# Zeroing a token table early in both of its rows, and adding the first-choice rows of h in PSUM for the last two expert pairs

## The reference

```python
def hier_moe(u, ...):                      # u = RMSNorm(h); 4 groups of 8 experts
    ...                                    # best group, then the best two experts in it
    top_w = softmax(top_logit) * g_w       # two weights per token
    hdn = silu(xb @ w1[e]) * (xb @ w3[e])  # per expert, on the tokens that chose it
    return (hdn @ w2[e]) weighted, summed over the token's two experts

def reference(x, ...):
    h = x
    for l in range(2):
        h = h + token_mixer(rms_norm(h, ln1_g[l]), ...)
        h = h + hier_moe(rms_norm(h, ln2_g[l]), ...)
    return rms_norm(h, final_g)
```

## Time and profile before

| | |
|---|---|
| median of 3 runs | 1402.55 us (1402.16 to 1403.12) |
| profiled execution, its own time | 1403.59 us |
| its span, first to last instruction | 1401.8 us |
| busy: PE, DVE, ACT, POOL | 97%, 32%, 32%, 35% |
| mean granted clock of TensorE | 0.991 |
| moved by DMA | 328.65 MB, mean 234 GB/s |

### The profile page before, as it was taken

How to read it: one execution, slowest core, us unless ns; L and a number is a source line. 1 busy time by engine, 2 the same in 40 slices (tenths; PEclk the granted TensorE clock), 3 DMA queues, 4 the chain that set the end, 5 groups by cost and what they waited for, 6 DMA issues and landing times.

```text
span 1401.8 us, 18500 instructions
## 1 busy us (share of the span) xinstructions
PE 1352.9 (97%) x7344; PEld 923.4 (66%) x7344; DVE 447.2 (32%) x991; ACT 453.4 (32%) x838; POOL 488.9 (35%) x239
## 2 busy tenths in 40 slices
PE   8999999999999999989999999999999999998987
PEld 7788777888887533333488887778888874333333
DVE  3333655100333421112336147541004252211124
ACT  5423576322232211111344236762223321111112
POOL 3625333565650111111044463246657301111101
PEclk9999999999999999999999999999999999999998
DMA  7612312235288999999963142222434889999997
GB/s 262 201 61 91 106 47 75 88 100 170 78 279 320 384 420 419 418 421 416 399 229 99 61 126 78 76 76 76 133 116 160 275 329 413 420 420 420 419 405 290
DMA packets 134069, 328.65 MB, mean 234 GB/s; under 512 B 16600, under 2 KB 96616, under 8 KB 111454
## 3 DMA queue, kind: packets, MB, share of 16 engines
q1 hardware_dynamic: 125342, 311.75, 59.4%
q0 software_dynamic: 8640, 15.69, 2.9%
HBM read 309.63 MB, written 33.55 MB: 245 GB/s over the span
## 4 chain that ended last, share of the span: by engine, by line
PE 78%; DMA 8%; DVE 4%; SPq 4%; ACT 3%; issue 1%; POOL 1%; DVEq 0%; POOLq 0%; ACTq 0%
PE ps L619 17%; PE ps L621 16%; PE ps L1053 16%; PE ps L620 16%; DMA w<-in_w 8%; SPq L511 3%; PE ps L849 1%; PE ps L856 1%; PE ps L1045 1%; PE ps L835 1%; DVE bT L1719 1%; PE ps L1065 1%; POOL ringL L1516 1%; PE ps L946 1%; PE ps L660 1%
## 5 line engine op out<-in xcount | busy, mean ns | idle before, releaser
L619 PE MATMUL ps<-uH,ringH 128*128 128x512 f32 x688 | 269.4, 392 | 0.0
L621 PE MATMUL ps<-uH,ringL 128*128 128x512 f32 x688 | 267.8, 389 | 0.0
L620 PE MATMUL ps<-uL,ringH 128*128 128x512 f32 x688 | 267.7, 389 | 0.0
L1053 PE MATMUL ps<-w,xT 128*64 128x512 f32 x1024 | 228.2, 598 | 5.0 <-DMA w<-in_w 4.3
L1053 PEld LDWEIGHTS ps<-w,xT 128*64 128x64 f32 x1024 | 73.8, 138 | 145.9 <-issue 138.1
L1516 POOL TENSOR_TENSOR ringL<-raw,ringH 128x2048 fp32r<-128x2048 f32 x28 | 129.6, 4635 | 101.2 <-ACT ringH L1208 101.2
L1053 PE MATMUL ps<-w,hT 128*64 128x512 f32 x512 | 124.6, 631 | 26.0 <-DMA w<-in_w 13.2
L1564 POOL TENSOR_TENSOR ringL<-raw,ringH 128x2048 fp32r<-128x2048 f32 x32 | 147.2, 4599 | 4.5 <-ACT ringH L1364 4.5
L619 PEld LDWEIGHTS ps<-uH,ringH 128*128 128x128 f32 x688 | 129.1, 188 | 27.8 <-issue 0.7
L621 PEld LDWEIGHTS ps<-uH,ringL 128*128 128x128 f32 x688 | 129.1, 188 | 26.9
L620 PEld LDWEIGHTS ps<-uL,ringH 128*128 128x128 f32 x688 | 129.2, 188 | 26.6
(11 more groups left out here) (306 smaller groups left out, 1996.4 us busy)
## 6 DMA issues: line engine op xcount, KB each, us to landing
w<-in_w SPq DMA_DIRECT2D x176, 1024.0 KB, 17.8
raw<-in_w_in SPq DMA_DIRECT2D x52, 1024.0 KB, 5.4
w<-in_w SPq DMA_DIRECT2D x32, 512.0 KB, 19.3
raw<-in_w_out SPq DMA_DIRECT2D x8, 1024.0 KB, 5.5
yb<-y_dram SPq DMA_DIRECT2D x8, 1024.0 KB, 16.7
braw<-in_w_branch SPq DMA_DIRECT2D x24, 256.0 KB, 4.6
h_dram<-hs SPq DMA_DIRECT2D x2, 2048.0 KB, 9.2
y_dram<-attT SPq DMA_DIRECT2D x8, 512.0 KB, 10.9
```

Source lines behind the costliest of these rows:

```text
L619: mm(o, h, rh, start=first, stop=False)
L620: mm(o, h, rl_, start=False, stop=False)
L621: return mm(o, l, rh, start=False, stop=last)
L1053: ins = mm(o[r], lhs[:, r], rhs[x], start=first, stop=last, skip_group_check=True)
```

## The change

1. The table is zeroed whole: the four transfers at unit 5 write both rows, 1 MB each, from all of `attT`.
2. `keep_rows` doesn't store h to `y_dram` any more; `rows_stored` and the two waits for it go. GpSimd's first scatter waits for `y_zeroed`.
3. For pairs 14 and 15 VectorE adds `xg * first_choice` to the product where it lies, in PSUM, one operation per bank. `last_rows` tells ScalarE, which waited for the down product itself before. In `pair(14)` both adds stand ahead of the masks, in `pair(15)` ahead of `last_out_low`.
4. `first_choice` becomes exactly 0 or 1 for every slot, an empty one too (`is_equal`), in as many operations as before.
5. The loop over overflow windows gets the same add and two more steps in its list.

```diff
@@ semaphores @@
-    y_zeroed = signal("y_zeroed", 16 * 4); y_stored = signal("y_stored", 16 * NS); rows_stored = signal("rows_stored", 16 * NT)
+    y_zeroed = signal("y_zeroed", 16 * 4); y_stored = signal("y_stored", 16 * NS); last_rows = signal("last_rows", 3)
@@ SyncE, unit 5 @@
-                        sp.dma_start(y_dram[2 * P * t:2 * P * (t + 1), :].rearrange("(p c) n -> p c n", c=2)[:, 1, :],
-                                     attT[:].rearrange("p h t i -> p (h t i)")[:, 0:D]).then_inc(y_zeroed.h, 16)
+                        sp.dma_start(y_dram[2 * P * t:2 * P * (t + 1), :].rearrange("(p c) n -> p (c n)", c=2),
+                                     attT[:].rearrange("p h t i -> p (h t i)")).then_inc(y_zeroed.h, 16)
@@ SyncE, keep_rows and behind @@
                 sp.dma_start(x_dram[t * P:(t + 1) * P, :], hs[:, t, :]).then_inc(u2_stored.h, 16)
-                sp.dma_start(y_dram[2 * P * t:2 * P * (t + 1), :].rearrange("(p c) n -> p c n", c=2)[:, 0, :], hs[:, t, :]).then_inc(rows_stored.h, 16)
...
             hold(sp, u2_stored.h, u2_stored.at(lay, 16 * NT))
-            hold(sp, rows_stored.h, rows_stored.at(lay, 16 * NT))
@@ ScalarE, pair @@
                 if p == NS:
-                    act.wait_ge(down_filled.h, down_filled.at(lay, p + 1))
+                    act.wait_ge(last_rows.h, last_rows.at(lay, 1))
                     fn(yH[0][:], ps[:, A[0] * 512:A[0] * 512 + 1024], ACT.Copy).then_inc(last_high.h, 1)
                     return
                 for c in range(2):
-                    act.wait_ge(last_down.h, last_down.at(lay, c + 1))
+                    act.wait_ge(last_rows.h, last_rows.at(lay, c + 2))
@@ GpSimd @@
-            hold(pool, rows_stored.h, rows_stored.at(lay, 16 * NT))
+            hold(pool, y_zeroed.h, y_zeroed.at(lay, 16 * NT))
@@ VectorE @@
+            def entry_places():
+                return v.scalar_tensor_tensor(first_choice[:], tokf[:], 2.0, bank(A[4])[:, 256 + NP:256 + 2 * NP], ALU.mult, ALU.subtract)
+
+            def choice_flags():
+                return v.tensor_scalar(first_choice[:], first_choice[:], float(SENT), None, ALU.is_equal)
+
+            def add_token_rows(rows, col, c):
+                o = bank(A[c])
+                return v.scalar_tensor_tensor(o, rows[:, c * 512:(c + 1) * 512], first_choice[:, col], o, ALU.mult, ALU.add)
...
-            link(v.scalar_tensor_tensor(first_choice[:], tokf[:], 2.0, bank(A[4])[:, 256 + NP:256 + 2 * NP], ALU.mult, ALU.subtract))
-            v.tensor_scalar(first_choice[:], first_choice[:], 1.0 - SENT, None, ALU.add)
+            link(entry_places())
+            choice_flags()
@@ VectorE, pair @@
                     dve.wait_ge(down_filled.h, down_filled.at(lay, p + 1))
+                    for c in range(2):
+                        last = add_token_rows(xg[p % 3], slice(p, p + 1), c)
+                    last.then_inc(last_rows.h, 1)
                     slot_tokens(tok_of[0], slice(p, p + 1)).then_inc(tokens_ready.h, 1)
...
                     sum_rows()
+                for c in range(2):
+                    dve.wait_ge(last_down.h, last_down.at(lay, c + 1))
+                    add_token_rows(xg[p % 3], slice(p, p + 1), c).then_inc(last_rows.h, 1)
                 last_out_low(0)
                 last_out_low(1)
```

More of the change, by code:

```diff
@@ L358, in trunk @@
     block = ctx.enter_context(nc.Block())
-    DVE_LINKS, ACT_LINKS, WIN_LINKS = 147, 2, 3
+    DVE_LINKS, ACT_LINKS, WIN_LINKS = 147, 2, 5
     dve_c = signal("dve_c", DVE_LINKS)
@@ L1486, in window_item @@
                 hold(act, win_down, n + 2)
+                hold(act, win_tokens, n + 1)
                 fn(yHw[:], ps[:, A[0] * 512:A[0] * 512 + 1024], ACT.Copy).then_inc(win_out_h, 1)
@@ L2146, in window_lists @@
                 chain(list_entries())
-                list_tokens().then_inc(win_lists, 1)
+                chain(list_tokens())
+                chain(entry_places())
+                choice_flags().then_inc(win_lists, 1)
                 hold(dve, win_lists, n + 1)
@@ L2153, in window_item @@
                 gated(ds(p, 1)).then_inc(win_hidden, 1)
+                hold(dve, win_down, n + 2)
+                for c in range(2):
+                    add_token_rows(xg[0], ds(p, 1), c)
                 slot_tokens(tok_w, ds(p, 1)).then_inc(win_tokens, 1)
```

## The result

The changed kernel takes 1405.13 us (median of 20 runs, 1402.09 to 1406.46) beside 1402.41 us for the kernel before on the same chip (20 runs): a ratio of 1.0018, 95% interval 1.0012 to 1.0024. It is slower by 2.7 us, where 2 us less were forecast. The profiled execution has a span of 1404.2 us against 1401.8.

What follows compares the result with a forecast made beforehand. The weight queue was taken to bound the expert stages, TensorE the rest. Removed stores -1.8 and -1.4, pair 15's adds +1.15, all else 0, gave -2.05 us: 1400.5 us from a median of 1402.55, range 1398.2 to 1405.0.

Steps and rivals of the forecast that it cites:

- What bounds the kernel: Each layer's expert stage ends when a full weight queue is worked off (419 GB/s); outside it TensorE is the bound.
- The removed store: Fourth store of h per layer, ahead of pair 2's weights: its removal gains 1.8 us in layer 0, 1.4 in layer 1.
- The waits that fell away: The two waits for `rows_stored`, on SyncE and ahead of GpSimd's first scatter: worth nothing.
- Against 4.8 us for an empty queue the lead is 2.1 us and 1.5 us: Weights issued at 490.57 and 1181.68: at most 2.1 and 1.5 us of lead can be carried past them.
- Rival B: Expert stage: queue gain lost, 0.5 us per layer left or less, tail costs 1.15; 1402.7 to 1403.7, chance 0.11.
- Pair 14's adds: Two VectorE operations of 745 ns ahead of ScalarE's copy; 1.5 us hidden before TensorE reads at 684.84: cost nothing.
- Pair 15's adds: On the path at each layer's end: subtraction 0 late by 0.5 us in layer 0, 0.65 in layer 1; 1.15 taken.
- three hand-overs more than I count: Upper bound for pair 15's adds over both layers: 2 us.
- The zeroing: Four 1 MB writes ahead of unit 6: 5.2 us at most at 406 GB/s, inside 6.7 us of slack, cost nothing.
- Rival A: Larger zeroing splits unit 6 late and TensorE waits in both layers: 1405.9, up to 1411; chance 0.17.
- The sum: Whole kernel: -1.8 - 1.4 + 1.15 + 0 = -2.05 us, median 1400.5.
- the term for the queue: Expert stages: gain from the removed store, -1.8 us in layer 0 and -1.4 in layer 1.

Runs made afterwards that it cites:

- a megabyte less early and late: Kernel before, one weight transfer per layer cut from 1 MB to 32 KB, at pair 4 (1402.21 us) or at pair 6 (1397.64 us).
- the stores put back: Changed kernel with the four stores of h per layer and their two waits restored, into a table nobody reads: 1403.74 us, ratio 1.0009.
- no adds: Changed kernel without the adds of the rows of pairs 14 and 15; ScalarE waits for the down product again: 1403.90 us, ratio 1.0009.
- rows put down early: Changed kernel, last pair's rows put into PSUM ahead of its down product, right behind pair 14's subtraction: 1403.70 us, ratio 1.0009.
- the move: Pair 3's first down weights issued behind pair 2's second instead of pair 5's: changed kernel 1402.05 us, kernel before 1402.12 us.
- the halves: Changed kernel, pair 5's first weights released and issued by halves, the first half some 3.4 us earlier: 1405.39 us, ratio 1.0021.
- rows put down late: Changed kernel, last pair's rows put into PSUM ahead of its down product, in layer 1 behind VectorE's sum of rows: 1413.01 us.

## Why the prediction was wrong, step by step

**What bounds the kernel.** Right: 1.02 and 419 GB/s from 505 to 660 us, and a megabyte less there is 2.4 us a layer.

**The removed store.** The first half was right in the main: a lead arose behind the empty queue at 457 us (0.6 MB), and pair 2's weights landed 5.5 us after issue in layer 1, as forecast, and 6.8 instead of 5.5 in layer 0. The waits that fell away are worth nothing, as forecast: SyncE issues on at 467.63 and GpSimd's first scatter starts at 485.50, 0.6 and 0.5 us earlier than in the kernel before, where all of the changed kernel is 0.5 us ahead. The step that failed is the next one: "Against 4.8 us for an empty queue the lead is 2.1 us and 1.5 us". The row that it was read from, 6.9 us at 490.57, is the last of sixteen completions. The trace records them all: on an empty queue (424.92) they come 4.3 to 4.8 us after issue, at 490.57 between 4.4 and 6.9, at 1181.68 between 4.5 and 6.3. So some DMA engines were done at these places in the kernel before as early as on an empty queue, while others were still busy. The lead over an empty queue was 0.1 us at the first engine and 0.9 and 0.4 us in the mean of the sixteen; the 2.1 and 1.5 us are those of the last one alone. The Trainium skill, DMA: Bandwidth & Descriptors, section "Why a DMA increments its semaphore by 16 and not by 1", says that the engines of one transfer finish independently and that only the full count means that all data has landed; these sixteen times agree. The runs with a megabyte less early and late show the consequence, 0.4 us in all and 2.4 us a layer, and the stores put back show it for the change itself. Whether the first engine or the mean sets what can be carried on is not shown: 0.1 us a layer and 1.3 us in all both lie within the interval of the run with less early. The prediction also looked for the tightest place in the kernel before alone; in the changed kernel the queue runs short at pair 4's weights first.

**What the prediction did not have at all** is the loss on top. The saving was not only cut to zero: with the tail taken away the changed kernel is still 1.4 to 1.5 us above the kernel before (no adds; rows put down early; each 1.0009, 1.0000 to 1.0018). Rival B had the gain lost and the tail staying, 1402.7 to 1403.7; the measured time lies 1.4 us above that, because B's worst case, "0.5 us per layer is left or less", ended at a gain of nothing and should have reached below zero: the stretches from 470 to 505 us run at 390 instead of 413 to 419 GB/s, and those from 1161 to 1197 at 374 to 385 instead of 409 to 416. A whole megabyte issued in the place of what was saved takes this loss away (the move); eight half-megabytes, four of them issued early, do not (the halves). Why the queue moves less there stays open.

**Pair 14's adds.** Right: 0.71 us each, and nothing moves.

**Pair 15's adds.** Right in mechanism, a little small in size: 0.58 and 0.84 us against 0.5 and 0.65; an add took 0.76 to 0.80 us instead of 0.745, and TensorE's wait for subtraction 0 is there. In layer 1 subtraction 1 ends at 1386.31, as late as forecast (1384.7, and all stands 1.6 us later by then), and the product that needs it starts 0.15 us behind that. The kernel before has the same 0.15 us (1383.91 and 1384.06), and the prediction left this hand-over out when it set the new end of the subtraction, 1384.7, against the old start of the product, 1384.06. The bound of "three hand-overs more than I count" was not needed.

**The zeroing.** Right: 416 GB/s against the 406 taken and the 313 needed, TensorE's wait still 0.36 us, and alone it changes nothing. Unit 6 lands 12.9 us after issue instead of 9.8, which spends 3.1 of the 6.7 us of slack. Rival A is out. The Trainium skill, DMA: Bandwidth & Descriptors, section "Latency and other measured facts", has copies with rows 512 KiB apart at 207 GB/s and with rows 4 MiB apart at 103. That does not carry down to the 8 KB here: the larger pitch is the slow one there, and in layer 1 the zeroing before runs at 420 GB/s from 732 to 734 us and only then falls to 223 and 206. Why it falls was not looked into.

**The sum.** -2.05 was -3.2 + 1.15. Measured are +1.2 (medians) to +1.4 (timelines) for the tail and, with it, +1.5 to +1.3 for the stage. So of the miss of 4.8 us, 4.5 to 4.7 are in the term for the queue, which had the wrong sign.

## What to carry to other kernels

Whether a saving in a queue can be carried on is decided at the next transfer that somebody else has to release. Look there at all sixteen completions and not at the landing alone: where the first ones come as on an empty queue, bytes saved ahead of that place brought next to nothing here. Then put another transfer in the place of the saved one; a transfer whose buffer is free but which stands behind one that waits is the first candidate. An add behind a product at the end could here be put down ahead of the product instead, but on an engine that works in order only ahead of that engine's own waits.

## What the runs showed of the hardware

A busy DMA queue is not a fast one: at shares from 0.97 to 1.01 the core moved between 374 and 419 GB/s. In the steady stream an 8 KB packet takes 309 ns; in the changed kernel from 487 to 503 us 118 of them took over 355 ns, up to 1.5 us, in the kernel before 28 from 486 to 505. What stretches them was not found: it goes with a queue that has just run short, but the run with halves had it with a full queue, and whether the smaller transfers did that there was not tried.

The end of the expert stage moves by up to 1.6 us from one execution to the next, between runs whose stage is nearly the same: against the kernel before, five kernels without the stores and without the move (changed, no adds, halves, rows put down late, rows put down early) ended it 0.86, 1.37, 0.57, 1.21 and -0.24 us late in layer 0. The verdicts on the stage therefore rest on medians, those on the tail also on timelines, where two profiles of the same tail agree to 0.06 us.
